# Weight sums of the second mixer: from accumulation in DRAM to additions on the chip

## What is computed

```
for i in range(DEPTH):                      # 2 layers
    xn = rmsnorm(h, norm_mix[i])
    h = h + (mlstm_mixer if i % 2 == 0 else diff_attn)(xn, ...)
    xn = rmsnorm(h, norm_ffn[i])
    h = h + swiglu(xn, ffn_w_in[i], ffn_w_out[i])

def diff_attn(xn, w_in, ...):
    proj = xn @ w_in                        # q, k, v: 3 x 1024 columns
    q, k = rope(rms(q, g_q)), rope(rms(k, g_k))
    s = einsum(q, k);  p = softmax(s)       # two score maps for each head
    a = p[:, :, 0] - lam * p[:, :, 1]
    o = rms(a @ v, g_sub) * (1 - lambda_init)
    return o @ w_out
```

## Time and profile before

| | us |
|---|---|
| median of 3 runs (lowest, highest) | 2004.11 (2002.53, 2007.06) |
| the profiled execution | 2001.02 |
| its span, first to last instruction | 1998.9 |
| mixer of layer 0 | 0 to 380 |
| feed-forward layer of layer 0 | 380 to 968 |
| seam: first fourteen products of the second mixer | 968 to 1050 |
| heads 0 to 7 with the other seventy products | 1050 to 1385 |
| output projection of the mixer | 1385 to 1450 |
| feed-forward layer of layer 1 | 1450 to 1999 |

### The profile page before, as it was taken

How to read it: one execution, slowest core, us unless ns; L and a number is a source line. 1 busy time by engine, 2 the same in 40 slices (tenths; PEclk the granted TensorE clock), 3 DMA queues, 4 the chain that set the end, 5 groups by cost and what they waited for, 6 DMA issues and landing times. The chain is left out here.

```text
span 1998.9 us, 31398 instructions
## 1 busy us (share of the span) xinstructions
PE 1895.7 (95%) x10741; PEld 1777.9 (89%) x10741; DVE 1256.6 (63%) x2120; ACT 926.9 (46%) x1989; POOL 1250.7 (63%) x1661
## 2 busy tenths in 40 slices
PE   9999999989968989999799999999899999999999
PEld 8888889989967989999788788887688999999998
DVE  6756657767643746577656666665568656657573
ACT  5443444454423434455534445544546454545453
POOL 4454453567745858687555555653157787878885
PEclk9999999989978989999878999987899999999999
DMA  7899997398899998743498987843333354443534
GB/s 251 275 234 236 242 221 213 114 245 229 219 233 235 237 259 231 227 125 97 153 228 213 217 165 148 174 106 66 95 96 102 107 148 121 121 143 98 155 113 131
DMA packets 419241, 350.88 MB, mean 176 GB/s; under 512 B 15835, under 2 KB 354558, under 8 KB 418838
## 3 DMA queue, kind: packets, MB, share of 16 engines
q1 hardware_dynamic: 381248, 266.39, 44.1%
q0 software_dynamic: 35712, 81.79, 22.8%
q10 hardware_dynamic: 2134, 0.82, 0.2%
HBM read 340.04 MB, written 172.48 MB: 256 GB/s over the span
## 5 line engine op out<-in xcount | busy, mean ns | idle before, releaser
L1234 PE MATMUL ps<-sx,wh 128*128 128x400 f32 (+1 forms) x2044 | 534.6, 343 | 25.8 <-ACT gt L2626 23.3
L1074 POOL TENSOR_TENSOR wl<-raw,wh 128x256 fp32r<-128x256 f32 (+1 forms) x432 | 353.9, 848 | 126.9 <-ACT wh L2611 125.6
L1234 PEld LDWEIGHTS ps<-sx,wh 128*128 128x128 f32 x2044 | 376.1, 189 | 29.3 <-ACT gt L2626 24.9
L1234 PE MATMUL ps<-sx,wl 128*128 128x400 f32 (+1 forms) x1022 | 349.5, 342 | 0.0
L1074 POOL TENSOR_TENSOR wl<-raws,wh 128x256 fp32r<-128x256 f32 x328 | 281.5, 898 | 100.7 <-ACT wh L2611 100.4
L1234 PE MATMUL ps<-fx,wh 128*128 128x400 f32 (+1 forms) x904 | 238.6, 345 | 12.4 <-POOL wl L1074 12.2
L2045 DVE TENSOR_TENSOR h<-h,ps 128x400 f32<-128x400 f32 (+1 forms) x280 | 153.9, 560 | 146.3 <-PE ps L1234 146.3
L1012 POOL CAST wh<-raw 128x256 fp32r<-128x256 f32 x156 | 66.1, 471 | 272.5 <-PE ps L1149 189.7
L1482 PE MATMUL ps<-sx,wh 128*128 128x400 f32 x672 | 212.0, 389 | 23.8 <-DVE v_raw L1960 11.5
L2611 ACT ACTIVATE wh<-raw 128x512 fp32r<-128x512 f32 (+2 forms) x268 | 142.5, 535 | 144.1 <-PE ps L1234 82.0
L1234 PEld LDWEIGHTS ps<-sx,wl 128*128 128x128 f32 x1022 | 193.5, 189 | 0.0
(11 more groups left out here) (384 smaller groups left out, 4163.2 us busy)
## 6 DMA issues: line engine op xcount, KB each, us to landing
in_sums<-in_ffn_w_in_dram SPq DMA_DIRECT2D x16, 1536.0 KB, 13.6
raw<-in_sums SPq DMA_DIRECT2D x96, 256.0 KB, 3.2
in_sums<-in_ffn_w_in_dram SPq DMA_DIRECT2D x16, 1280.0 KB, 10.0
raw<-in_ffn_w_in_dram SPq DMA_DIRECT2D x80, 256.0 KB, 3.0
raws<-in_sums SPq DMA_DIRECT2D x80, 256.0 KB, 3.2
raw<-out_sums SPq DMA_DIRECT2D x120, 128.0 KB, 2.5
raws<-in_ffn_w_in_dram SPq DMA_DIRECT2D x52, 256.0 KB, 3.3
raw<-in_m_w_in_dram SPq DMA_DIRECT2D x24, 512.0 KB, 5.7
```

What stands on the lines that cost most here:

```text
L1074: ins = pool.tensor_tensor(slot_of(n, 1)[:, c], raw_of(n)[:, c], slot_of(n, 0)[:, c].bitcast(F32), ALU.subtract)
L1234: mm = pe.matmul(product_bank(layer, s, j), slot_of(n, low_w)[:, k * P:(k + 1) * P], x, start=(j in OPENS and k + q == 0), stop=(k == tile ...
```

## The change

1. `kv_sums`, `q_sums` and their sixteen transfers are gone. SP loads quarter blocks (60 loads, four for each set) into eight buffers: four raw, two `mix_sums`, two `mix_more`. A table `FACTOR` says for each product which buffer holds its factor, which blocks are loaded for it and which sums are made; POOL makes the 51 sums as additions of buffers (`factor_sums`, two instructions each, L1118).
2. ScalarE makes the high parts of all 84 products (L2841), in the heads by `mix_highs(hd, i)` at six places of a head. POOL keeps the low parts (L1129).
3. The four first products (kv and q, j = 0 and 3) are opened together: k tiles 0 to 2 of all four, then k tile 3. Afterwards come the kv products and then those of q. Three products (was two) stand ahead of head 0.
4. ScalarE waits only for six of the eight stores of h, and behind its first copy; the buffers of queries and transposed probabilities move to other tiles of h.
5. The eight `LATER_COPIES` are added to `NEXT_COPIES`: all 24 copies for the second feed-forward layer stand in the first one.
6. Evacuations: in the heads VectorE adds kv 4 ahead of the end of the rotary step; in head 6, which makes fewer products, these are spread over more places, and the splits of y are spread over heads 6 and 7; the outputs are turned in two parts, each with its own signal.

```diff
-MIX_ORDER = [(kind, 0, j) for j in KV_ORDER for kind in ("kv", "q")]
+MIX_ORDER = [("kv", 0, 0), ("q", 0, 0), ("kv", 0, 3), ("q", 0, 3), *(("kv", 0, j) for j in (2, 1, 4, 5, 6)),
+             *(("q", 0, j) for j in (2, 1, 4, 5, 6))]
+N_OPENED, N_AHEAD = 4, 3
...
-NEXT_COPIES = (*range(12, 17), *range(20, 25), *range(28, 34))
-LATER_COPIES = {14 + 4 * i: 16 + i for i in range(8)}
+NEXT_COPIES = (*range(5, 9), *range(12, 17), *range(20, 25), *range(28, 38))
-MIX_COPIES = {1: 0, 2: 1, 3: 2, 4: 3, 6: 4, 7: 5, 8: 6, 9: 7}
-MIX_ADDS = {(12, 0): 0, (13, 0): 1, (15, 0): 2, (17, 0): 3, (20, 0): 4, (21, 0): 5, (23, 0): 6, (25, 0): 7}
...
+                        ins = pool.tensor_tensor(weight_buffer(dst)[:, c], weight_buffer(a)[:, c], weight_buffer(b)[:, c], ALU.add)
+                    ins.then_inc(mix_summed if n == len(sums) - 1 else mix_part, 1)
 
             def mix_parts(m):
 
-                if m >= N_FIRST:
-                    pool.wait_ge(mix_raw_in[m % 4], 16 * (m // 4 + 1))
-                    pool.wait_ge(mix_done, m - 3)
-                    for c in pieces(KP * P):
-                        ins = pool.tensor_copy(mix_weight(m, 0)[:, c], mix_raw(m)[:, c])
-                    ins.then_inc(mix_hi, 1)
+                for n in (m, m + 1):
+                    if n < N_MIX and FACTOR[MIX_ORDER[n]][2] and sums_before(n) == m:
+                        factor_sums(n, m)
+                src = weight_buffer(FACTOR[MIX_ORDER[m]][0])
                 pool.wait_ge(mix_hi, m + 1)
...
+            for k0, k1 in ((0, KP - 1), (KP - 1, KP)):
+                for x in MIX_ORDER[:N_OPENED]:
+                    mix_product(x, k0, k1)
...
                 if not last:
+                    if not short:
+                        add("kv", 4)
                     rope_end(1, kx, hd + 1)
-                    add("kv", 4)
...
+                src = FACTOR[MIX_ORDER[m]][0]
+                if loads_until(m, src):
+                    sc.wait_ge(mix_raw_in[src], loaded(src, loads_until(m, src)))
+                if SUMS_MADE[m]:
+                    sc.wait_ge(mix_summed, SUMMED + SUMS_MADE[m])
+                sc.activation(mix_weight(m, 0), weight_buffer(src), ACT.Copy).then_inc(mix_hi, 1)
...
                 exps(hd, odd, 2)
+                if not last:
+                    mix_highs(hd, 0)
                 squared(hd, odd, 0)
...
                 exps(hd, odd, 3)
+                if not last:
+                    mix_highs(hd, 1)
                 squared(hd, odd, 1)
...
-            sc.wait_ge(h_last_stored, IN_ONCE + 16 * KT)
-            for m in range(N_FIRST - 4):
+            for m in range(N_FIRST):
                 mix_high(m + 4)
+                if m == 1:
+                    sc.wait_ge(h_last_stored, IN_ONCE + 16 * 2 * (KP - 1))
```

## The result

The changed kernel takes 2030.15 us (median of four runs, 2027.45 to 2031.23), the kernel before 2003.32 us (four runs, 1995.13 to 2007.06): a ratio of 1.0138, with a 95% interval of 1.0104 to 1.0171. It is slower, where 1988 us had been forecast; the time lies above the range that was given, 1948 to 2026.

The account below looks back on a forecast made before the run. TensorE was taken to bound the kernel, only its idle time and clock being at stake. −51 − 9 + 52 − 8.7 = −16.7 us from 2001.0 gives 1984.3, with 3.1 added 1987, rounded up to 1988 us; range 1948 to 2026.

Parts of the forecast that it names:

- Feed-forward layer, −51: First feed-forward layer: waits behind DRAM sum transfers and the low clock after them go, −51 us, bounds −57 and −30.
- Seam, −9: Seam: two TensorE waits, 10.3 us, go and one POOL sum of 1.46 us comes on the path, −9 us.
- The upper bound of +3: Seam: the holes only change their releaser and two POOL sums, 2.9 us, come in front, +3 us.
- Heads, +52: Heads: eleven waits behind ScalarE's high parts 48.9 us, clock 15, less 11.5 us, +52 us; bounds +15 and +86.
- 7.55 + 2.22 = 9.8 us after the end of 39: Head 2: when product 41's weights are ready; TensorE wants them after 5.3 us, so a second wait of 4.5 us.
- The term for q 5: Heads, upper bound: three sums of an odd head's q 5, 4.4 us of POOL, three heads, put some 10 us on top.
- The clock, +15: Heads: clock loss of 2.5 us after each hole, taken for 6 of 11 holes, 15 us.
- v_raw, −11.5: Heads: seven waits for the addition of kv 4 ahead of the last kv product go, −11.5 us.
- Tail, −8.7: Before the output projection: 6.2 us waiting for y's split tiles and one 2.5 us clock fall go, −8.7 us.
- The contention that the rivals put at 1.28 us: POOL: low parts on the path take 1.28 instead of 0.73 us, 2001 us in all; chance 0.05.
- slower, by the heads: Heads: high parts waiting for POOL sums hold up ScalarE's copies and TensorE, +86 us, 2022 us in all; chance 0.15.
- Slower, by the transfers: Feed-forward layer: second-layer copies keep half of the holes, −30 us and 5 us more waits, 2014 us; chance 0.13.

Follow-up runs that it names:

- the last experiment: Changed kernel with POOL making the high parts of products 18 to 83, plus the eight late copies back in the mixer: 1932.4 us against 1933.28 without that move.

## Why the prediction was wrong

**Feed-forward layer, −51, came −57.3.** The mechanism was right. Of the ten us left standing, the four for short waits stayed (4.2 us of idle time) and the six for the new copies did not come: in either place these cost nothing, as the last experiment confirms. The lower bound of −57 was the value.

**Seam, −9, came +19.6: the largest miss, 28.6 us.** The step that failed is the price of what takes the old waits' place: a sum is 1.46 us, "and I put one on the path". The two old waits went in the main: the 4.7 us for the inputs' factors are gone, and the 5.6 us for ScalarE's copy are 3.5. But the new waits were not looked for far enough down ScalarE's order. High parts stand there in front of the squares of the queries and of the first exponentials, and they wait for loads, or for sums that wait for loads: 5.3 us at 972 us, and 15.6 instead of 3.4 us ahead of the second scores. Another 3.1 us for h and 2.0 us for v_raw came in. Idle time is 29.8 instead of 15.0 us. One product more stands in the seam (2.3 us), and the rest is clock, 0.75 instead of 0.82 on average. The upper bound of +3 priced the POOL instructions but not the transfers ahead of the loads.

**Heads, +52, came +68.3,** or +72.6 when the wait for y's tile is left to the tail. The two waits a head, their releaser, their places and their number (6 + 5) were right. The first was sized at 4.4 and measured at 4.02. The failed step is the second one: "7.55 + 2.22 = 9.8 us after the end of 39" counts ScalarE and POOL alone and takes the weights as loaded. In odd heads product q 5 needs four loads, whose buffers the preceding low part frees, and three sums. Together the waits gave 68.6 instead of 48.9 us. The term for q 5 was named in the upper bound (10 us), but as POOL's sums only; the runs showed 24 us beyond the pure place, of which 19.7 go when the accumulating transfers are issued one product later. The 4.7 that stay, a good 1.5 in each odd head, are left for the three sums. No term of the sum had either part.

**The clock, +15, came as nothing.** TensorE was busy for 345.0 us in the heads, before for 345.9. It had been at a mean clock of 0.89 there before and was at 0.88 after. In the kernel before with ScalarE's high parts TensorE was busy for 15.6 us longer, beside holes of the same kind. In the feed-forward layer, where the price of 2.5 us a hole was read, the clock's part came nearly as booked: up to the seam TensorE was busy for some 12 us less (12.6 had been estimated). In the heads the size of this term is thus unsettled. That it was booked on top of stretches already slow may have been the error; no run tests it.

**v_raw, −11.5,** went as forecast, but 5.2 us more of waits for the key roots and 4.3 us more for another VectorE result came. **Tail, −8.7, came −8.3,** of which the cuts show 4.0 behind the heads and 4.3 in them. This term was right: the 6.2 us for y's tiles fell to 1.0, and TensorE was busy for 3.0 us less, at a clock of 1.00 in the first 10 us of the output projection where it had been 0.70. **POOL:** additions took 0.73 us:

```profile
L1118 POOL TENSOR_TENSOR mix_sums<-mix_sums,raw x42: 721/732/1069, 924.8 to 1393.3; 128x256 f32<-128x256 f32 x42
```

The contention that the rivals put at 1.28 us an instruction did not show on the path: the five low-part instructions behind the wait of 9.75 us in head 3 took 3.47 us, 0.69 each. The section Key points of the Trainium skill's GPSIMD Engine Reference says that POOL shares its SBUF interfaces with VectorE and names this contention. The trace shows at most rare cases of it: 1.07 us is the longest of these 42 additions, and their median is 0.73.

**The rivals.** The one that came nearest is "slower, by the heads": ScalarE's strict order, waits for a sum, and what is queued behind them, with 2022 us against 2030. It decided at heads of over +68, where they were; it had a chance of 0.15. It had been described right and put into the heads alone, while the larger part of the miss, 28.6 of 43 us, came in the seam. "Slower, by the transfers" is refuted: it placed its waits in the feed-forward layer, and there 57 us went. It was other transfers, the accumulating ones beside the mixer, that made loads late.

## What to carry to other kernels

When a producer's step is moved to an engine that also carries a latency chain, write down for each moved instruction what it waits for and what stands behind it there, back to the load and the buffer that the load needs; price that chain, not the instruction's 0.63 us. An engine with plenty of idle time, as ScalarE with 46%, can be the wrong home, while POOL at 71% in the heads held TensorE up for 1.8 us in all. And a change with two parts is best judged in halves: here the change without the moved high parts is worth some 60 us, nearly all of it by the transfers that left, and the moved high parts cost some 90.

## What was not expected of the hardware

- A load of 256 KB issued 0.2 us behind an accumulating transfer of 1280 KB landed after 11.3 us, and after 4.6 us when the transfer was issued later. Loads issued 0.1 us behind such a transfer landed after 2.7 to 4.8 us, those 0.2 to 4.1 us behind it with the transfer, after 8.5 to 13.5 us. Where the border lies is not settled: with the transfers one product later, one load 0.5 us behind still took 3.4 us, and two others 10.7 and 12.8. Over the seam and the heads of the changed kernel 56 loads of quarter blocks take 2.7 to 13.5 us, with a median of 4.0.
- The same instructions in the same heads took 371.0 and 358.5 us, by TensorE's busy time alone (345.9 and 331.5 us, granted clock 0.89 and 0.94), in the kernel before with and without its sums in DRAM. What the holes 400 us earlier have to do with that stays open.
- The kernel before varies from 1983 to 2007 us over its runs, the one with POOL's high parts from 14 on only from 1926.5 to 1929.7.
